# The first output projection by column halves instead of by token tiles, on one core

## The reference

```python
        merged = jax.nn.sigmoid(gate_a) * ya + jax.nn.sigmoid(gate_g) * yg
        x = x + jnp.einsum('bsd,de->bse', merged, w_out[l])

        h2 = rmsnorm(x, norm2_w[l])
        x = x + expert_choice_ffn(h2, w_router[l], w_gate[l], w_up[l], w_down[l])
...
def expert_choice_ffn(h, w_router, w_gate, w_up, w_down):
    logits = jnp.einsum('bsd,de->bse', h, w_router).astype(jnp.float32)
    aff = jax.nn.softmax(logits, axis=-1)
    top_val, top_idx = lax.top_k(jnp.swapaxes(aff, 1, 2), cap)
    xs = jax.vmap(lambda hb, ib: hb[ib])(h, top_idx)
    gt = jnp.einsum('becd,edf->becf', xs, w_gate)
    up = jnp.einsum('becd,edf->becf', xs, w_up)
    ye = jnp.einsum('becf,efd->becd', jax.nn.silu(gt) * up, w_down)
```

## Time and profile before

| what | us |
|---|---|
| median of 3 runs | 2345.04 |
| the profiled execution's own time | 2345.38 |
| its span in the trace | 2343.6 |
| `out_proj` begins on PE | 956.37 |
| `out_proj` ends, last logits begin | 1017.50, 1021.11 |
| first expert matmul on PE | 1046.41 |
| last ring slab's issue by SP | 1926.90 |
| DMA rate from 1110 to 1949 us | 428 GB/s |

### The profile page before, as it was taken

How to read it: one execution, slowest core, us unless ns; L and a number is a source line. 1 busy time by engine, 2 the same in 40 slices (tenths; PEclk the granted TensorE clock), 3 DMA queues, 4 the chain that set the end, 5 groups by cost and what they waited for, 6 DMA issues and landing times. The chain is left out here.

```text
span 2343.6 us, 29638 instructions
## 1 busy us (share of the span) xinstructions
PE 2182.5 (93%) x12225; PEld 1195.8 (51%) x12225; DVE 948.6 (40%) x1625; ACT 532.2 (23%) x989; POOL 236.3 (10%) x194
## 2 busy tenths in 40 slices
PE   8999999999999999969999898989898988999998
PEld 5875554467767768644343333333333324455544
DVE  2457757756776655240101010101010102457864
ACT  1446644422232241010000000000000002233323
POOL 1420000133333303000000000000000000022000
PEclk9999999999999999979999999999999999999999
DMA  7221010011011142439999999999999997221210
GB/s 248 72 78 34 35 37 19 9 46 29 20 33 33 29 154 108 188 136 401 427 428 427 428 427 429 427 428 427 428 428 427 428 429 280 76 73 37 77 54 36
DMA packets 94120, 488.13 MB, mean 208 GB/s; under 512 B 9957, under 2 KB 36995, under 8 KB 68899
## 3 DMA queue, kind: packets, MB, share of 16 engines
q1 hardware_dynamic: 93987, 486.25, 51.3%
HBM read 482.82 MB, written 3.41 MB: 207 GB/s over the span
## 5 line engine op out<-in xcount | busy, mean ns | idle before, releaser
L1787 PE MATMUL PS<-R 128*64 128x512 f32 x1024 | 230.4, 597 | 32.6 <-DMA R<-w_up 23.6
L1787 PE MATMUL PS<-SL,R 128*64 128x512 f32 x1024 | 227.2, 595 | 26.4 <-DMA SL<-w_gate 18.9
L2098 DVE TENSOR_TENSOR HT<-HT,PS 128x512 f32<-128x512 f32 x32 | 20.6, 684 | 366.2 <-PE PS L1787 366.2
L2402 PE MATMUL PS<-HT,SL 128*128 128x512 f32 x384 | 168.6, 594 | 0.0
L1787 PEld LDWEIGHTS PS<-SL,R 128*64 128x64 f32 x1024 | 72.7, 137 | 178.2 <-issue 128.7
L1787 PEld LDWEIGHTS PS<-R 128*64 128x64 f32 x1024 | 70.0, 137 | 181.6 <-issue 125.9
L2103 DVE COPY HT<-PS 64x512 f32<-64x512 f32 x16 | 10.9, 683 | 303.8 <-PE PS L1817 303.8
L1816 PE MATMUL PS<-SL,HT 128*64 128x512 f32 x256 | 114.4, 594 | 13.5 <-ACT HT L1929 6.2
L1816 PE MATMUL PS<-R,HT 128*64 128x512 f32 x256 | 114.3, 594 | 12.5 <-ACT HT L1929 7.0
L2402 PEld LDWEIGHTS PS<-HT,SL 128*128 128x128 f32 x384 | 72.2, 190 | 87.2 <-issue 86.1
L796 PE MATMUL PS<-HT,SL 128*128 128x512 f32 x256 | 114.1, 600 | 0.8 <-PEq L557 0.8
(11 more groups left out here) (446 smaller groups left out, 3712.4 us busy)
## 6 DMA issues: line engine op xcount, KB each, us to landing
R<-w_gate SPq DMA_DIRECT2D x32, 2048.0 KB, 35.4
SL<-w_gate SPq DMA_DIRECT2D x32, 2048.0 KB, 33.6
SL<-w_up SPq DMA_DIRECT2D x32, 2048.0 KB, 32.6
R<-w_up SPq DMA_DIRECT2D x32, 2048.0 KB, 33.0
SL<-w_down SPq DMA_DIRECT2D x31, 2048.0 KB, 35.4
R<-w_down SPq DMA_DIRECT2D x28, 2048.0 KB, 27.8
SL<-w_in SPq DMA_DIRECT2D x18, 2048.0 KB, 8.5
X<-w_in SPq DMA_DIRECT2D x16, 512.0 KB, 3.8
```

The lines of the kernel that those rows point to most:

```text
L1787: m = pe.matmul(banks[n][half * CAP:(half + 1) * CAP, :], XC[x // 2 % 2][:, 2 * j + k, toks], w[:, k, (2 * half + n) * 512:(2 * half + n + ...
L2098: tt(H[:, j, :], SG[j], UB[j][:, :], ALU.mult).then_inc(E7["h"], 1)
L2402: m = pe.matmul(bank_[:, :], slab(i % 2)[:, k, j * P:(j + 1) * P], hT[:, k, :], start=(k == 0), stop=(k == KD - 1))
```

## The change

The units of `out_proj` are renumbered: unit u is now tile u % 4 and half u // 4, so that the four left halves come first and the four right halves after them. The waits, PE's order, ACT's and DVE's counts follow. SP's wait ahead of slab r = 5 is for `m5` at 4 in place of 8, and the wait for 8 stands ahead of r = 6. PE's new order is: units 0 to 3 (left), unit 4, unit 5, turn 0, unit 6, logits 0, turn 1, unit 7, logits 1, turn 2, logits 2, turn 3, logits 3. DVE adds the four left halves first, and then does for each tile: one residual add, the copy, the wait for `rstd`, the `h2` write.

```diff
@@ SP
                     elif r == 5:
+                        sp.wait_ge(m5, NT)
+                    elif r == 6:
                         sp.wait_ge(m5, 2 * NT)
@@ PE
                 def out_proj(u):
-                    t, n = u // 2, u % 2
+                    t, n = u % NT, u // NT
...
-                    pe.wait_ge(merge5, KD - 1 if u < 2 else KD)
+                    pe.wait_ge(merge5, KD - 1 if t < 2 and n == 0 else KD)
...
                 def turn_x(t):
-                    pe.wait_ge(out5, 2 * t + 2)
+                    pe.wait_ge(out5, NT + t + 1)
...
+                for u in range(NT):
+                    out_proj(u)
                 for t in range(NT):
-                    out_proj(2 * t)
+                    out_proj(NT + t)
+                    if t > 1:
+                        logits(t - 2)
                     if t:
                         turn_x(t - 1)
-                    out_proj(2 * t + 1)
-                    if t:
-                        logits(t - 1)
+                logits(NT - 2)
                 turn_x(NT - 1)
                 logits(NT - 1)
@@ ACT
-                    act.wait_ge(out5, 2 * t + 2)
+                    act.wait_ge(out5, NT + t + 1)
@@ DVE
+                def residual5(u):
+                    t, n = u % NT, u // NT
+                    xs = x3[:, t, n * 512:(n + 1) * 512]
+                    dve.wait_ge(m5, u + 1)
+                    v(tt(xs, xs, PS[u % 4][:, :], ALU.add), out5)
+
+                for u in range(NT):
+                    residual5(u)
                 for t in range(NT):
-                    for n in range(2):
-                        u = 2 * t + n
-                        xs = x3[:, t, n * 512:(n + 1) * 512]
-                        dve.wait_ge(m5, u + 1)
-                        v(tt(xs, xs, PS[u % 4][:, :], ALU.add), out5)
+                    residual5(NT + t)
```

## The result

| timed together | kernel before, us | changed kernel, us | ratio, 95% interval |
|---|---|---|---|
| first session | 2345.22 (6 runs) | 2353.84 (6 runs, 2350.01 to 2354.74) | 1.0033 [1.0023, 1.0043] |
| second | 2346.83 (33) | 2349.77 (11) | 1.0011 [1.0002, 1.0020] |
| fourth | 2345.89 (27) | 2350.00 (11) | 1.0020 [1.0011, 1.0029] |

(In the third session only the kernel before and variants were timed.) The changed kernel is slower. How much depends on the session: the forecast of 2349.0 lies 4.8 us under the first and 0.8 and 1.0 under the others. All runs pooled (a third profile of the changed kernel, 2351.20, among them) give a median of 2346.19 for 104 runs of the kernel before, between 2343.06 and 2351.00 (one run at 3498.95, with a mean granted clock of 0.609, stands alone and is left out), and 2350.54 for 29 of the changed one, between 2348.71 and 2354.74. That is 4.35 us.

A forecast was written before the change was run, and what follows sets the result against it. It took the expert layer to be paced by DMA slabs, its start set by the chain from projection to first expert matmul. Early slab 0, tail 1.9 and clock 2.1 sum to 4.0 us: 2349.0 us, range 2344.8 to 2351.0.

The forecast's parts named there:

- What bounds the kernel: Expert layer: slabs move at the DMA's pace; PE, DVE and ACT's chain from projection to first expert matmul sets its start.
- the early slab at 0: SP's slab 5 leaves some 34 us earlier, gaining 0; bounds 0 and 4.9 us of gain.
- PE's order up to turn 2: PE from the projection's start: waits are covered, turn 2 starts at 1016.45, and the projection ends 2.75 us earlier.
- The tail, +1.9: Behind turn 2: turn 3 waits for DVE's late add of unit 7, +1.9 us; bounds 0.7 and 2.9.
- a bound of its clock term: Upper bound of 2.9 us for the clock's cost: logits 2 runs low as well and ends 0.8 late.
- its own sign of being wrong: Wrong if turn 3 does not wait for DVE, or the first expert matmul or the experts' end is not later.
- The clock, +2.1: Tail: PE's clock falls ahead of turn 3, slowing it by 0.8 and logits 3 by 1.3; bounds 0 and 2.9.
- The clock's return: Near the gather and first expert step: PE's high clock returns unmoved, 0, plus or minus 1.5 us.
- The sum on the median: Whole kernel: 4.0 us passed on one to one, 2349.4 on the profiled execution, 2349.0 on the median.

The follow-up runs named there:

- e1: The changed kernel with slab 5 waiting for all eight units again; 2351.81 us, ratio 1.0018 to the kernel before.
- e6: The kernel before with slabs 5, 6 and 7 held back until PE's softmax transposes; 2345.99 us, ratio 0.9997.
- e7: The kernel before with slabs 5, 6 and 7 held back until the top 64; 2348.22 us, ratio 1.0012.
- e4: The changed kernel with unread matmuls added where PE waits; 2345.03 us, ratio 1.0000 to the kernel before.
- e3: The changed kernel with DVE adding unit 7 directly behind turn 2's copy and PE doing turn 3 ahead of logits 2; 2347.25 us, ratio 1.0010 to the kernel before.

## Why the prediction was wrong, point by point

- **What bounds the kernel, and the early slab at 0.** Right. The slab left at 986.91 (forecast 984, plus the 2.88 us of a later start), the DMA was empty before the ninth slab, and e1, e6 and e7 bound the slack from both sides.
- **PE's order up to turn 2.** Right to 0.05 us: 60.13 against 60.08.
- **The tail, +1.9.** Right: 1.79 where the clock was still high (e4), 1.78 in two of the changed kernel's own profiles. In the other two, the first and the fourth, turn 3 came 2.5 and 2.1 us late and did not wait for DVE: logits 2, at the low clock, ended last. The prediction had that only as a bound of its clock term, and its own sign of being wrong, a turn 3 that does not wait for DVE, is met there.
- **The clock, +2.1.** Right in kind and size. It fell ahead of turn 3 in all four profiles. At the first expert matmul all four together are 3.8 to 4.6 us late, 4.1 in the mean (94.19 - 90.06), of which the tail's order is 1.8 and the clock 2.3. The longest idle time of PE between turn 2 and logits 3 was 0.84 us. The page "TensorE: Matmul & The Clock Gate" of the Trainium skill, in "HAM oscillation", has longer idle gaps of PE lower the clock. By that rule alone the clock would have stayed up; the trace does not agree, and the measurement decides here.
- **The clock's return, 0 with plus or minus 1.5.** Held in two profiles out of four. In the first profile the first opening step ran at the low clock in part: 3.81 us from 1053.91 to 1057.72 against 3.01. The ninth slab was then 5.4 us late, and the same in the fourth, against 4.1 and 3.8 in the second and third.
- **The sum on the median, and the range: here it failed.** "On the median, 0.34 lower, 2349.0" put the 4.0 us on 2345.04, the median of three runs that lay within 0.6 us, and the range up to 2351.0 held only the unknowns of the changed stage. The time outside the changed stage stood in the sum at nothing, without a reason, and the clock's return at 0. Neither was so in the first session's profile, 9.4 us longer than the one before where 4.0 were forecast. The path from the projection to the ninth slab took 5.4 us more: turn 3 was 2.5 late (forecast 1.9), 2.1 were added from there to the first expert matmul (forecast 2.1), and 0.8 by the opening step at the low clock (forecast 0). Outside it 2.88 us were lost before the projection: 1.7 by a longer low stretch near 325 (windows of 315 to 330, 0.66 where the kernel before had 0.77), 1.7 near 855 (windows of 850 to 860), less 0.5 by which this execution was ahead before its first 100 us were over. All of that is unchanged code. Another 1.1 came behind the ninth slab. The kernel before runs anywhere from 2343 to 2351, and the changed one from 2349 to 2355. Of the first six runs of the changed kernel five lay above 2353, of the 23 later ones two. The difference between the pooled medians, 4.35 us, is near what the sum had forecast, 4.0; by the four profiles it is 4.7 at the ninth slab. The first session's 8.6 was that and about as much again. That this was the luck of the draw is not shown: the kernel before, with 22 of its 98 later runs above 2349, had none of its six above 2346.51 in that session. Only one of the five slow runs was profiled; the other four share its mean clock, 0.988.

What stays open: what decides in which executions the clock falls near 855 us. The three profiles in which it did (2354.74, e4's 2350.31, e7's 2353.17) are all among the slower executions of their kernels, and none of the other eleven shows it. Open too is why five of six runs of the first session were of that kind.

## What to carry to other kernels

A buffer that comes free sooner was worth nothing measurable here, because its transfer had long landed when the next could be issued; look for an empty DMA ahead of that point before spending an order of work on it. Splitting a stage by columns first makes each row tile complete later, so all that needs whole tiles crowds behind the last unit, in the in-order queues of every engine; lay out that tail by hand, because here its arrangement was nearly the entire loss on the path (e3). And before trusting three runs as a base, take a dozen: the spread of a kernel is in its untouched parts too.

## What the runs showed of the hardware

- PE's granted clock can fall while PE is at work. In the tail it went from 1.00 to 0.50 with idle times of 0.84 us at most, PE having done logits, a turn and part of the next logits.
- Unread matmuls in PE's waits held the clock at 1.00 over 20 us of DVE work and made the kernel 3.0 us faster, ratio 0.9983 [0.9973, 0.9992]. Placed behind a fall they cost: 1.74 us for two issued matmuls against 1.02.
- Two executions of the same kernel can differ by more than 4 us in 2350: of the changed kernel's profiled runs, 2354.74 and 2350.55 are 4.2 us apart, 2.6 of it ahead of the projection (of which 1.7 at the low stretch near 855, in unchanged code) and 1.3 from there to the ninth slab.
- What the low clock costs in one and the same stage varies with the execution, counted from the projection's start: the changed kernel's four profiles have the ninth slab at +95.84 to +97.44.
